# A hybrid decoder layer on one core: the bias table's load and products moved to the head of the program, and the fourth tile's transposes half a block sooner

## What is computed

```python
h = rmsnorm(x, norm_pre_mix[l])
proj = jnp.einsum('bsd,de->bse', h, w_in[l])
hq, hf, hi, hg, aq, ak, av, iq, ik, iw = jnp.split(proj, PROJ_SPLITS, axis=-1)
y_a = hgrn2_mixer(hq, hf, hi, hg, lb_all[l], hgrn_gnorm[l])
y_b = dsa_mixer(..., iq.reshape(B, S, IDX_HEADS, IDX_DIM), ik, iw, rel_bias)
y = jnp.einsum('bse,ed->bsd', jnp.concatenate([y_a, y_b.astype(y_a.dtype)], axis=-1), w_o[l])
x = x + rmsnorm(y, norm_post_mix[l])
h = rmsnorm(x, norm_pre_ffn[l])
ff = jax.nn.silu(jnp.einsum('bsd,df->bsf', h, w_gate[l])) * jnp.einsum('bsd,df->bsf', h, w_up[l])
ff = jnp.einsum('bsf,fd->bsd', ff, w_down[l])
x = x + rmsnorm(ff, norm_post_ffn[l])
```

## Time and profile before

| | |
|---|---|
| median of 3 runs | 664.31 us (664.03 to 665.09) |
| the profiled execution | 664.47 us |
| its span, first to last instruction | 662.7 us, so 1.8 us lie around it |
| PE busy | 652.5 us, 98% |
| DVE, ACT, POOL busy | 535.2 us (81%), 343.6 us (52%), 91.8 us (14%) |
| granted TensorE clock, mean | 0.999 of full |
| share of the chain that ended last | PE 94%, DVE 2%, ACT, issue and DMA 1% each |

### The profile page before, as it was taken

How to read it: one execution, slowest core, us unless ns; L and a number is a source line. 1 busy time by engine, 2 the same in 40 slices (tenths; PEclk the granted TensorE clock), 3 DMA queues, 4 the chain that set the end, 5 groups by cost and what they waited for, 6 DMA issues and landing times.

```text
span 662.7 us, 10171 instructions
## 1 busy us (share of the span) xinstructions
PE 652.5 (98%) x4029; PEld 582.1 (88%) x4029; DVE 535.2 (81%) x746; ACT 343.6 (52%) x547; POOL 91.8 (14%) x131
## 2 busy tenths in 40 slices
PE   8999999999999999999999999999999999999996
PEld 6878888888888889888998999999999998888885
DVE  5766999998988768345986988989989879987845
ACT  5656433443349578234653555554555565644532
POOL 4800230000405378002100000000000000000000
PEclk9999999999999999999999999999999999999999
DMA  8443042343521300262342323334234235444513
GB/s 277 129 159 100 29 128 65 96 158 96 190 65 64 121 7 19 110 191 64 98 157 63 105 87 128 93 101 128 77 115 128 68 108 207 158 148 153 164 45 127
DMA packets 50946, 75.01 MB, mean 113 GB/s; under 512 B 5329, under 2 KB 40145, under 8 KB 50642
## 3 DMA queue, kind: packets, MB, share of 16 engines
q1 hardware_dynamic: 47040, 62.26, 29.6%
q0 software_dynamic: 3568, 11.55, 4.7%
q10 hardware_dynamic: 290, 0.55, 0.2%
HBM read 69.60 MB, written 6.84 MB: 115 GB/s over the span
## 4 chain that ended last, share of the span: by engine, by line
PE 94%; DVE 2%; ACT 1%; issue 1%; DMA 1%; POOL 0%; DVEq 0%; POOLq 0%; SPq 0%; ACTq 0%
PE PS L1626 38%; PE PS L1966 27%; PE PS L2004 12%; PE PS L2015 4%; PE PS L1845 2%; PE PS L1700 2%; PE PS L1676 1%; PE PS L1675 1%; PE PS L1856 1%; PE PS L1779 1%; PE PS L1670 1%; DMA A<-in_x_dram 1%; PE PS L1741 1%; PE PS L1710 1%; ACT A L905 1%
## 5 line engine op out<-in xcount | busy, mean ns | idle before, releaser
L1626 PE MATMUL PS<-hT_lo,w_hi 128*128 128x512 f32 (+2 forms) x280 | 102.0, 364 | 0.0
L1626 PE MATMUL PS<-hT_hi,w_hi 128*128 128x512 f32 (+2 forms) x280 | 100.7, 360 | 0.0
L1626 PE MATMUL PS<-hT_hi,w_lo 128*128 128x512 f32 (+2 forms) x280 | 100.7, 359 | 0.0
L1085 DVE TENSOR_TENSOR w_lo<-raw,w_hi 128x2048 fp32r<-128x2048 f32 x21 | 48.1, 2291 | 19.0 <-ACT w_hi L726 18.8
L1966 PE MATMUL PS<-hT_hi,W_r 128*128 128x256 f32 x216 | 61.1, 283 | 0.0
L1966 PE MATMUL PS<-hT_hi,s_w 128*128 128x256 f32 x216 | 61.1, 283 | 0.0
L1966 PE MATMUL PS<-hT_lo,s_w 128*128 128x256 f32 x216 | 61.1, 283 | 0.0
L1626 PEld LDWEIGHTS PS<-hT_hi,w_hi 128*128 128x128 f32 (+1 forms) x280 | 52.5, 188 | 8.4
L1626 PEld LDWEIGHTS PS<-hT_lo,w_hi 128*128 128x128 f32 (+1 forms) x280 | 52.6, 188 | 7.3 <-issue 0.2
L1626 PEld LDWEIGHTS PS<-hT_hi,w_lo 128*128 128x128 f32 (+1 forms) x280 | 52.6, 188 | 7.2
L1966 PE MATMUL PS<-s_t,s_w 128*128 128x256 f32 x288 | 57.8, 283 | 0.6 <-ACT PS L954 0.6
(11 more groups left out here) (306 smaller groups left out, 1685.9 us busy)
## 6 DMA issues: line engine op xcount, KB each, us to landing
raw<-in_w_in_dram SPq DMA_DIRECT2D x15, 1024.0 KB, 5.5
W_f<-in_w_gate_dram SPq DMA_DIRECT2D x9, 1024.0 KB, 5.3
W_f<-in_w_up_dram SPq DMA_DIRECT2D x9, 1024.0 KB, 5.3
W_f<-in_w_down_dram SPq DMA_DIRECT2D x16, 512.0 KB, 3.5
raw<-in_w_o_dram SPq DMA_DIRECT2D x4, 1024.0 KB, 4.9
W_f<-in_w_down_dram SPq DMA_DIRECT2D x3, 1024.0 KB, 4.9
A<-in_x_dram SPq DMA_DIRECT2D x4, 512.0 KB, 6.0
A<-in_x_dram POOLq DMA_DIRECT2D x4, 512.0 KB, 5.6
```

Of the source, the lines that this page charges most:

```text
L1085: dve.tensor_tensor(lo, raw_view(j), hi.bitcast(F32), ALU.subtract).then_inc(s_lo, 1)
L1626: o = pe.matmul(out, lhs[a], rhs[b], start=(first and n == 0), stop=(last and n == 2))
```

## The change

The bias table and the one-hot matrix are issued from ACT's queue, right behind the gain row, with a semaphore of their own (`s_tab`), and no longer from SP's. Their products stand on PE right behind the gain row's, in PSUM banks 0 and 1 in place of 6 and 7; of nine transposes of `keep_busy` behind them two are left. ACT copies the result between the squares of the second tile and the first `turn_hi`. PE waits for that copy (`s_gsb`) ahead of the second `keep_busy`, since bank 1 is written there. `turn_in(3)` is called between the two halves m of `first_rows(1, m, ...)` instead of behind both. SP has one more wait (`s_lo_half`) ahead of the load of chunk 3, and DVE waits for two small loads in place of four. `s_eps` is declared and not used.

```diff
@@ sync
-            sp.dma_start(tab, rel_bias).then_inc(s_small, 16)
-            sp.dma_start(oh_sb, onehot).then_inc(s_small, 16)
...
+                if ring_of(j) == 2:
+                    sp.wait_ge(s_lo_half, 1)
@@ scalar
             act.dma_start(gain_row, norm_pre_mix).then_inc(s_gin, 16)
+            act.dma_start(oh_sb, onehot).then_inc(s_tab, 16)
+            act.dma_start(tab, rel_bias).then_inc(s_tab, 16)
...
             square_in(1)
+            act.wait_ge(s_gps, 1)
+            act.activation(g_sb[:, 0:S], PS[0:HEADS_B, 0, :], ACT.Copy)
+            act.activation(g_sb[:, S:S + P], PS[0:HEADS_B, 1, 0:P], ACT.Copy).then_inc(s_gsb, 1)
             turn_hi(0, TURN_BANK[0], 0)
...
             split(1)
-            act.wait_ge(s_gps, 1)
-            act.activation(g_sb[:, 0:S], PS[0:HEADS_B, 6, :], ACT.Copy)
-            act.activation(g_sb[:, S:S + P], PS[0:HEADS_B, 7, 0:P], ACT.Copy).then_inc(s_gsb, 1)
@@ vector
-            dve.wait_ge(s_small, 64)
+            dve.wait_ge(s_small, 32)
@@ tensor
             o.then_inc(s_gps0, 1)
-            keep_busy(1, 9)
+            pe.wait_ge(s_tab, 32)
+            pe.matmul(PS[0:HEADS_B, 0, :], tab, oh_sb[:, 0:S], start=True, stop=True)
+            pe.matmul(PS[0:HEADS_B, 1, 0:P], tab, oh_sb[:, S:S + P], start=True, stop=True).then_inc(s_gps, 1)
+            keep_busy(7, 2)
             turn_in(0)
             turn_in(1)
+            pe.wait_ge(s_gsb, 1)
             keep_busy(1, 8)
...
-            for m in range(2):
-                first_rows(1, m, first_hi, hT_hi)
+            first_rows(1, 0, first_hi, hT_hi)
             turn_in(3)
+            first_rows(1, 1, first_hi, hT_hi)
...
-            pe.wait_ge(s_small, 64)
-            pe.matmul(PS[0:HEADS_B, 6, :], tab, oh_sb[:, 0:S], start=True, stop=True)
-            pe.matmul(PS[0:HEADS_B, 7, 0:P], tab, oh_sb[:, S:S + P], start=True, stop=True).then_inc(s_gps, 1)
```

More of the change, by code:

```diff
@@ L224, in hymba_layer @@
         s_small = sem("small_landed")
+        s_tab = sem("bias_table_landed")
+        s_eps = sem("epsilon_set")
         s_raw = [sem(f"raw_landed{i}") for i in range(2)]
```

## The result

The changed kernel takes 666.07 us in the median of 14 runs (664.13 to 666.28), the kernel before 664.37 us in as many (663.78 to 665.12). The ratio is 1.002, 95% interval 1.0013 to 1.0027: slower by 1.7 us between the medians, by 0.9 to 1.8 us by the interval. The forecast was 663.4 us, 0.14% faster. The runs of the changed kernel don't scatter around one value: ten of the fourteen lie between 665.8 and 666.3, the others at 664.1, 664.2, 664.7 and 665.1.

The account below looks back on a forecast made before the run. PE was taken to bound the kernel, with work nearly all the time, so gains in the head count where PE is the chain. Terms: -1.15 + 0.25 = -0.90 us, giving 663.4 us for the median; range 662.7 to 664.8.

Parts of the forecast that it names:

- The products leave the end of the head, and the fourth tile's transposes come sooner: PE at the head's end: first product of the last two tiles at 19.86 instead of 21.01, gaining 1.15 us.
- The split: Head's end: of the products' 1.17 us, 0.63 gained and 0.54 turned into a wait for hT_lo without sooner transposes.
- The bytes: DMA in the head: 80 KB beside the first tiles delay the second tile's landing by 0.25 us, bounds 0 and 0.5.
- The rule of turns between queues: Each DMA engine alternates between queues packet by packet, so the full 0.25 us is paid: 663.4, otherwise 663.2.
- The wait for the table: PE at the head's front: table there at 3.5 to 6.1 us, level with 5.99; harmless until 7.45 us.
- ACT's additions: ACT in the head: two issues of some 0.5 us each and 0.74 us of copies fit its idle time; nothing.
- SP: SP's queue: two issues fewer, and the added wait is met long before SP comes there; nothing.
- the stretch behind the head: Second chunk's w_lo is ready at 23.19 us and PE wants it at 26.0, so nothing eats the gain.
- The table's products at the front: PE behind the gain row's products: 1.17 us plus 0.30 for two transposes, hidden by 0.89 us idle; small either way.
- Rival 4: PE's clock rises later because seven transposes give way to products of 8 columns and 32 rows: 665.4 us, chance 0.05.
- The range: Stated range of the measured time: 662.7 to 664.8 us, with 0.3 us added on either side for spread of runs.
- own range: The forecast's 663.1 to 664.1 us, from 0.63 to 1.17 us gained and 0 to 0.5 paid; chance 0.64.

Follow-up runs that it names:

- without the second edit: Changed kernel with table's products padded by zeros to the whole array, fourth tile's transposes back behind both halves: 665.56 us, ratio 1.0013.
- the second edit alone: Kernel before with only the fourth tile's transposes moved between the halves of first_rows: 664.67 us, ratio 1.0003.
- padded: Changed kernel with the table's products on the whole array, zeros around the table and the one-hot matrix: 665.12 us, ratio 1.0008.
- interleaved: Changed kernel with the narrow product cut into five of 128 columns, transposes behind each (pairs behind four, one behind the last): 669.51 us, ratio 1.0078.
- behind nine transposes: Changed kernel with table's products zero-padded to the whole array, nine transposes ahead of the wait for the table, none behind its products: 663.74 us, ratio 0.9989.
- the first experiment: Kernel before with two unread products of 32 rows by 8 columns replacing seven of nine transposes, no load moved: 666.99 us, ratio 1.0034.

## Why the prediction was wrong

- *The products leave the end of the head, and the fourth tile's transposes come sooner: 1.15 us.* Right: 1.10 us in the trace. The split was right too: the wait for `hT_lo` without the second edit is 0.46 us (forecast 0.54), and the second edit alone gives nothing.
- *The bytes: 0.25 us.* Not refuted. The loads moved alone give 664.57 against 664.32 us, ratio 1.0003 [0.9994, 1.0011], which neither shows 0.25 us nor excludes it. The second tile's square began 0.10 us later in the changed kernel's trace than before, but 6.27 us was late for a kernel with the loads on SP's queue: the six such traces have it at 5.79 to 6.27 us (median 5.90), the ten with the loads on ACT's at 6.09 to 6.65 us (median 6.41). The rule of turns between queues stays unproved: the table landed at 6.9 us, after 5.2 us, later than from SP's queue (4.1 to 4.3 us), so it did not jump the line as I argued from the gain row, which was itself used 1.7 to 2.9 us behind its issue, differing from trace to trace.
- *The wait for the table: level with 5.99.* It landed at 6.9, ahead of PE only because the gain row was late as well; where it came later still, in the padded and the interleaved versions, PE waited 0.28 to 0.62 us for it. With the transposes put ahead of the wait its price is below what the medians tell (663.44).
- *ACT's additions, SP, the stretch behind the head: nothing.* Right; the 1.55 us at 22.56 us are the 1.5 of the spans.
- *The table's products at the front: hidden, "Small either way".* **This is the step that failed.** I saw that the gain row's products ran at half pace, and I took the rise at 5.99 us as given: a moment that stays where it is when the work around it changes. I then priced the low pace for the two products and two transposes alone (0.2 us at most behind them) and not for the sixteen transposes behind. In the runs the rise came late with narrow products in front, and all that PE did until about 13.7 us was at the low pace: 2.65 us, on the path, the late gain row's 0.90 us included, since the idle gaps of 0.89 and 0.36 us that were to hide it are smaller. The experiments name the step: unread products of the table's shape in front give the loss with no load moved (666.99 us), and without the products the rest of the sum gives 663.44. Rival 4 named this mechanism and gave 665.4 us; it got a chance of 0.05 because the rise was seen at 5.99, ahead of the nine transposes, which seemed to prove that they don't matter. Their 0.13 us each was a mean: the first came at 0.213 us, the low pace, and the second at 0.187. One trace can't prove that, as it shows one execution and one moment.
- *The range.* The own range plus 0.3 us on either side is 662.8 to 664.4 us; the sum gives no reason for the 664.8 that was stated. The measured 666.07 lies outside either.

What stays open: how much of the padded version's remaining loss (665.12 against 663.74 behind nine transposes) is the idle time ahead of the table and how much the smaller amount of work before it; the two were changed together. Open too is what it is in the products that counts, their rows and columns or the values that move through them, and whether a late gain row adds to the loss. That wide work ahead helps and the same work behind doesn't (664.12 against 667.14 us with narrow products) is shown.

## What to carry to other kernels

A warm-up stretch is part of the schedule: work whose results nobody reads may be what brings TensorE to its full pace, and the products of few rows or few columns tried here were no replacement for it, even when they took as long. Put such products behind the wide work, and time the version (padding alone gave back a part here, 665.12 us): a trace of one execution tells the pace of one execution. And where a forecast says "hidden at either pace", price everything that would run at the low pace until the rise, not the moved instructions alone.

## What the runs showed that I had not expected

- Unread products of 32 rows by 8 columns, 97 by 8, or 32 by 128 at the program's start cost time (666.3 to 667.1 us), those of 97 by 128 did not (664.8 us). In the traces of 32 by 128 and of the table's own products with no wide work ahead PE stayed at half its pace until 12.7 to 15.3 us, in that of 97 by 128 until 9.3.
- The pace can fall again soon after its rise, without a long idle gap: at full pace from 5.69 us until about 8.6 with 0.89 us of idle time, at half (granted clock 0.50) from 8.6 to 12.0 (the first experiment's trace).
- The granted clock of the stretch ahead of the first rise is noted as 1.00 while the same transposes take twice as long (one every 0.213 us against one every 0.109).
- PE's first use of the gain row varies by 1.25 us (from 2.49 to 3.74 us), and comes late with the moved loads and without them.
